# Sums of values in the first attention: rounded operands, values as rounded and remainder columns, two query tiles per matmul

## The reference, cut to what matters

```python
# q, k, v: [1, 512, 16, 64]; for each block of queries, over the keys before its end
log_fail = where(mask, log_sigmoid(-logits), 0.0)
between  = cumsum(log_fail, reverse=True) - log_fail
w        = where(mask, exp(log_sigmoid(logits) + between), 0.0)
out      = einsum('bhqk,bkhd->bqhd', w, v)
...
y_sb = einsum('ble,ed->bld', o * silu(z_sb), w_sb_proj)
```

## Time and profile before

| what | value |
|---|---|
| median of 3 runs | 1355.64 us (1355.26 to 1355.69) |
| profiled execution: its time | 1355.3 us |
| profiled execution: span | 1353.4 us |
| TensorE busy, share of the span | 99% |
| VectorE, ScalarE busy | 60%, 46% |
| attention stage | about 301.6 to 470.8 us |
| granted TensorE clock | 1.00 in all slices |

### The profile page before, as it was taken

One profiled execution on the slowest core, in us unless ns is written; L12 is line 12 of the kernel. 1 busy time (PEld: TensorE's weight loads), 2 busy tenths in 40 slices (PEclk: granted clock), 3 DMA queues, 4 the chain that ended last, 5 costly groups with the idle time before them and its releaser, 6 DMA issues. The chain is left out here.

```text
span 1353.4 us, 17944 instructions
## 1 busy us (share of the span) xinstructions
PE 1338.7 (99%) x6941; PEld 1111.6 (82%) x6941; DVE 818.6 (60%) x1271; ACT 620.9 (46%) x1147; POOL 53.8 (4%) x38
## 2 busy tenths in 40 slices
PE   9999999999999999999999999999999999999998
PEld 7888878888888888888778877888898888888886
DVE  5786654357666544343648876667464565656668
ACT  6554433457767633323526466663443332333333
POOL 0025300000000000000010000000000000000000
PEclk9999999999999999999999999999999999999999
DMA  4222113242111154322261200101425312331321
GB/s 169 85 82 84 63 63 112 90 129 90 32 63 49 56 208 136 106 86 87 73 198 52 84 23 17 32 1 59 151 88 176 135 34 92 134 116 63 104 84 62
DMA packets 33621, 120.67 MB, mean 89 GB/s; under 512 B 3716, under 2 KB 5124, under 8 KB 32258
## 3 DMA queue, kind: packets, MB, share of 16 engines
q1 hardware_dynamic: 32962, 118.48, 26.1%
q10 hardware_dynamic: 576, 1.05, 0.4%
HBM read 112.18 MB, written 4.19 MB: 86 GB/s over the span
## 5 line engine op out<-in xcount | busy, mean ns | idle before, releaser
L1004 PE MATMUL bank<-a_hi,whi 128*128 128x512 f32 (+1 forms) x880 | 346.7, 394 | 0.4 <-DVE a_lo L2402 0.4
L1004 PE MATMUL bank<-a_hi,wlo 128*128 128x512 f32 (+1 forms) x880 | 336.8, 383 | 0.0
L1004 PE MATMUL bank<-a_lo,whi 128*128 128x512 f32 (+1 forms) x880 | 335.9, 382 | 0.0
L1452 ACT ACTIVATE whi<-wraw 128x1024 fp32r<-128x1024 f32 x170 | 175.9, 1055 | 194.2 <-PE bank L1004 125.9
L1835 DVE TENSOR_TENSOR wlo<-wraw,whi 128x1024 fp32r<-128x1024 f32 x170 | 206.9, 1233 | 63.3 <-ACT whi L1452 59.7
L1004 PEld LDWEIGHTS bank<-a_hi,wlo 128*128 128x128 f32 x880 | 165.4, 188 | 33.0
L1004 PEld LDWEIGHTS bank<-a_hi,whi 128*128 128x128 f32 x880 | 165.8, 188 | 31.5 <-issue 2.3
L1004 PEld LDWEIGHTS bank<-a_lo,whi 128*128 128x128 f32 x880 | 165.8, 188 | 31.2 <-issue 1.7
L1004 PE MATMUL bank<-arena 128*128 128x128 f32 (+5 forms) x1332 | 185.9, 285 | 1.9 <-DVE arena L2393 1.1
L1004 PEld LDWEIGHTS bank<-arena 128*128 128x128 f32 (+1 forms) x1332 | 165.0, 191 | 11.8 <-issue 5.3
L1004 PE MATMUL bank<-whi,a_hi 128*128 128x512 f32 x288 | 115.0, 399 | 1.4 <-DVE wlo L1835 0.7
(11 more groups left out here) (269 smaller groups left out, 1838.0 us busy)
## 6 DMA issues: line engine op xcount, KB each, us to landing
wraw<-in_wblk SPq DMA_DIRECT2D x170, 512.0 KB, 3.9
arena<-in_quarters SPq DMA_DIRECT2D x8, 1024.0 KB, 8.4
arena<-in_quarters SPq DMA_DIRECT2D x4, 768.0 KB, 6.3
arena<-in_x SPq DMA_DIRECT2D x4, 512.0 KB, 6.1
arena<-in_x SPq DMA_DIRECT2D x1, 2048.0 KB, 8.2
spill<-arena SPq DMA_DIRECT2D x4, 512.0 KB, 7.5
arena<-spill SPq DMA_DIRECT2D x1, 2048.0 KB, 9.4
out<-arena SPq DMA_DIRECT2D x8, 256.0 KB, 2.0
```

What stands on the lines that cost most here:

```text
L1004: return nc.tensor.matmul(o, lhsT, rhs, start=start, stop=stop, **kw)
L1452: A(whi[n % 2][:, cols], wraw[i][:, 0:cols.stop - cols.start], ACT.Copy).then_inc(s_hi, 1)
```

## The change

The sums of values get rounded operands. For each head the 64 columns of values become 128 columns of weights, 64 rounded and 64 remainder (values_of(h)); the turned weights are split too, into sb_wT_hi, which ScalarE writes with its copy, and sb_wT_lo, which VectorE gets by subtracting it from the same bank. Two query tiles are summed together: in even units of TensorE, function summed does a matmul of 256 columns for every block of keys that both tiles see and one of 128 for the last block, each for hi and lo. The output then has 64 rows from rounded values and 64 from remainders, which ScalarE and VectorE add. TensorE's order in a unit changes: sums, turns, logits. ScalarE copies the turned weights first in a unit, VectorE subtracts first. The turns wait for s_wTlo (VectorE) where they waited for s_wT (ScalarE). The last three units are woven with slices of the first z_sb block. One DMA (the residual) waits for half the count of s_pv, which now counts pairs. Memory places change.

```diff
@@ -227,9 +227,12 @@
     for c in range(NK):
         gs += feature("gate_ssd", [(G0 + P * c, P), (P * c, P)], [("gate", c), ("y_ssd", c)], "AB")
     steps += weave([("sb", u) for u in range(SH * NT)], gs)
-    steps += [("sb", SH * NT + i) for i in range(SB_LAG + 1)]
     for j in range(4):
-        steps += feature("w_in", [(ZS0 + 256 * j, 256)], [("z_sb", 2 * j), ("z_sb", 2 * j + 1)], "AA")
+        zs = feature("w_in", [(ZS0 + 256 * j, 256)], [("z_sb", 2 * j), ("z_sb", 2 * j + 1)], "AA")
+        if j == 0:
+            for i in range(SB_LAG + 1):
+                zs.insert(2 * i + 1, ("sb", SH * NT + i))
+        steps += zs
     for c in range(NK):
         steps += feature("gate_sb", [(G0 + D + P * c, P), (P * c, P)], [("gate2", c), ("y_sb", c)], "AB")
         if 1 <= c <= NK // 2:
@@ -694,8 +697,7 @@
 
         def k_hihi(h):
 
-            i = h // 2
-            kb = (30, 28, 30)[h] if h < 3 else 72 + 2 * (i - 1) if h % 2 else 28 if i == 2 else 72 + 2 * (i - 3)
+            kb = 78 if h >= 13 and h % 2 else 30 - 2 * (h % 2)
             return mem(kb, [T], rounded_arena)
 
         def head_rows(h):
@@ -716,8 +718,18 @@
         ones_r = b_hi[:, 5, 0:P]
         sb_sig = mem(48, [2, T])
         sb_fail = mem(52, [2, T])
-        sb_w = mem(57, [3, T])
-        sb_wT = mem(63, [2, T])
+        sb_w = mem(56, [3, T])
+        sb_wT_hi = mem(64, [NT, 2 * P], rounded_arena)
+        even_values = mem(62, [NT, P], rounded_arena)
+        odd_values = mem(32, [NT, D], rounded_arena)
+
+        def sb_wT_lo(h):
+            return mem(24 if h < SH // 2 else 72, [NT, 2 * P], rounded_arena)
+
+        def values_of(h):
+
+            return odd_values[:, :, P * (h // 2):P * (h // 2) + P] if h % 2 else even_values
+
         v_before = [mem(52, [NT, 512]), mem(16, [NT, 512])]
         small_t = {"dt": mem(12, [T]), "gates": mem(10, [T])}
         tt = mem(48, [2, T])
@@ -829,6 +841,7 @@
         s_dv = sem("s_value_steps")
         s_vs = [sem(f"s_values_shifted{i}") for i in range(2)]
         s_tr, s_wT, s_pv, s_o = sem("s_sb_turned"), sem("s_sb_wT"), sem("s_sb_summed"), sem("s_sb_out")
+        s_orest, s_wTlo, s_vhi, s_vlo = sem("s_sb_out_rest"), sem("s_sb_wT_rest"), sem("s_values_rounded"), sem("s_values_rest")
         s_khi, s_klo, s_kz = sem("s_stacks_rounded"), sem("s_stacks_rest"), sem("s_stacks_zero")
         s_t, s_tround, s_mg = sem("s_product"), sem("s_product_rounded"), sem("s_merged")
         s_res, s_zero = sem("s_residual"), sem("s_zero")
@@ -907,6 +920,19 @@
 
         def norm_no(name, t):
             return APPLIED.index((name, t)) + 1
+
+        def value_head(u):
+
+            if u == 0:
+                return 0
+            return u // NT + 1 if u % NT == NT - 1 and u // NT + 1 < SH else None
+
+        def summed_head(u):
+
+            o = u - SB_LAG - 2
+            if u == SH * NT + SB_LAG:
+                return SH - 1
+            return o // NT if 0 <= o and o % NT == NT - 1 else None
 
         def norm_cols(name, t):
 
@@ -962,7 +988,7 @@
                     sp.wait_ge(s_xd, 2 * NT)
                     sp.dma_start(rows["y"], dram["ssd_norm"]).then_inc(s_row["y"], 16)
                 if n == LATE:
-                    sp.wait_ge(s_pv, SH * NT)
+                    sp.wait_ge(s_pv, SH * NT // 2)
                     sp.dma_start(xres, by_token(dram["x"])).then_inc(s_res, 16)
                     sp.dma_start(npost, dram["norm_post"]).then_inc(s_res, 16)
                 if n == LATE + 2:
@@ -1351,6 +1377,17 @@
                                 .then_inc(s_aux, 1)
 
             def stick(u):
+                v = u - SB_LAG - 1
+                if 0 <= v < SH * NT and v % 2:
+                    summed(*divmod(v, NT))
+                v = u - SB_LAG
+                if 0 <= v < SH * NT:
+                    pe.wait_ge(s_scan, v + 1)
+                    if v >= 1:
+                        pe.wait_ge(s_wTlo, v)
+                    for kb in range(v % NT + 1):
+                        last = nc.tensor.transpose(bank[BANK_WT][:, P * kb:P * kb + P], sb_w[:, v % 3, P * kb:P * kb + P], ident)
+                    last.then_inc(s_tr, 1)
                 if u < SH * NT:
                     h, qt = divmod(u, NT)
                     kend = P * (qt + 1)
@@ -1366,29 +1403,25 @@
                     mm(ps[:, 0:kend], queries, k_hihi(h)[:, 0:kend], True, False)
                     mm(ps[:, 0:kend], queries, k_lo[:, h % 2, 0:kend], False, False)
                     mm(ps[:, kend - P:kend], identb, strict, False, True).then_inc(s_qk, 1)
-                v = u - SB_LAG
-                if 0 <= v < SH * NT:
-                    pe.wait_ge(s_scan, v + 1)
-                    if v >= 1:
-                        pe.wait_ge(s_wT, v)
-                    for kb in range(v % NT + 1):
-                        last = nc.tensor.transpose(bank[BANK_WT][:, P * kb:P * kb + P], sb_w[:, v % 3, P * kb:P * kb + P], ident)
-                    last.then_inc(s_tr, 1)
-                v = u - SB_LAG - 1
-                if 0 <= v < SH * NT:
-                    h, qt = divmod(v, NT)
-                    pair = slice(P * (h // 2), P * (h // 2) + P)
-                    pe.wait_ge(s_wT, v + 1)
-                    if qt == 0:
-                        pe.wait_ge(s_dv, 1 + h // 8)
-                        if h == 1:
-                            pe.wait_ge(*end_sem("v"))
-                        if h >= 2:
-                            pe.wait_ge(s_o, h - 1)
-                    for kb in range(qt + 1):
-                        last = mm(bank[BANKS_STICK[h % 2]][:, P * qt:P * qt + P], vt[:, kb, pair],
-                                  sb_wT[:, v % 2, P * kb:P * kb + P], kb == 0, kb == qt)
-                    last.then_inc(s_pv, 1)
+
+            def summed(h, qt):
+
+                pe.wait_ge(s_wT, NT * h + qt + 1)
+                pe.wait_ge(s_wTlo, NT * h + qt + 1)
+                if qt == 1:
+                    pe.wait_ge(s_vlo, h + 1)
+                    if h == 1:
+                        pe.wait_ge(*end_sem("v"))
+                    if h >= 2:
+                        pe.wait_ge(s_o, h - 1)
+                out_ = bank[BANKS_STICK[h % 2]]
+                passes = [(kb, half) for half in (sb_wT_hi, sb_wT_lo(h)) for kb in range(qt + 1)]
+                passes.append(passes.pop(qt + 1))
+                for n, (kb, half) in enumerate(passes):
+                    first = P if kb == qt else 0
+                    last = mm(out_[:, P * (qt - 1) + first:P * qt + P], values_of(h)[:, kb, :], half[:, kb, first:2 * P],
+                              n == 0, n == len(passes) - 1)
+                last.then_inc(s_pv, 1)
 
             for s in STEPS:
                 if s[0] == "gemm":
@@ -1595,7 +1628,25 @@
                 if i == 2:
                     A(q_hilo[own, h % 2, :], qf[own, h // 2, :], ACT.Copy).then_inc(s_khi, 1)
 
+            def round_values(h):
+
+                if h % 2 == 0:
+                    act.wait_ge(s_dv, 1 + h // NH)
+                    if h >= 2:
+                        act.wait_ge(s_pv, 2 * (h - 1))
+                else:
+                    act.wait_ge(s_vlo, h)
+                A(values_of(h)[:, :, 0:HD], vt[:, :, HD * h:HD * h + HD], ACT.Copy).then_inc(s_vhi, 1)
+
             def stick(u):
+                v = u - SB_LAG
+                if 0 <= v < SH * NT:
+                    kend = P * (v % NT + 1)
+                    act.wait_ge(s_tr, v + 1)
+                    if v >= 2 and v % 2 == 0:
+                        act.wait_ge(s_pv, v // 2)
+                    A(sb_wT_hi[:, 0:v % NT + 1, P * (v % 2):P * (v % 2) + P],
+                      bank[BANK_WT][:, 0:kend].rearrange("p (a b) -> p a b", b=P), ACT.Copy).then_inc(s_wT, 1)
                 if u < SH * NT:
                     kend = P * (u % NT + 1)
                     act.wait_ge(s_qk, u + 1)
@@ -1608,13 +1659,12 @@
                     A(sb_fail[:, u % 2, 0:kend], ps[:, 0:kend], ACT.Sigmoid, scale=-SCALE).then_inc(s_sig, 1)
                     if u % NT < 3 and u // NT + 1 < SH:
                         stack(u // NT + 1, u % NT)
-                v = u - SB_LAG
-                if 0 <= v < SH * NT:
-                    kend = P * (v % NT + 1)
-                    act.wait_ge(s_tr, v + 1)
-                    if v >= 2:
-                        act.wait_ge(s_pv, v - 1)
-                    A(sb_wT[:, v % 2, 0:kend], bank[BANK_WT][:, 0:kend], ACT.Copy).then_inc(s_wT, 1)
+                if value_head(u) is not None:
+                    round_values(value_head(u))
+                h = summed_head(u)
+                if h is not None:
+                    act.wait_ge(s_pv, 2 * h + 2)
+                    A(qf[HD * (h % 2):HD * (h % 2) + HD, h // 2, :], bank[BANKS_STICK[h % 2]][HD:P, :], ACT.Copy).then_inc(s_orest, 1)
 
             def dt_part(i):
 
@@ -1887,6 +1937,10 @@
                     if kind == "y_ssd":
                         if i == 0:
                             dve.wait_ge(s_dv, 2)
```

(26 more changed lines are left out.)

## The result

| | before | after |
|---|---|---|
| median | 1355.36 us | 1362.25 us (1360.98 to 1363.19, 5 runs) |
| ratio | | 1.0049, 95% interval 1.0034 to 1.0064 |
| profiled execution, its span | 1355.3, 1353.4 us | 1363.19, 1361.4 us |
| one round of the attention stage | 21.03 us | 21.51 us |

The account below looks back on a forecast made before the run. TensorE, busy for 99% of the span, was taken as the bound. First round +1.8, six rounds +2.6, last round -0.3, end -1.0, small waits +0.2 gave +3.3 on 1355.3: 1358.6, by the median 1359.0; range 1347 to 1365.

Parts of the forecast that it names:

- that case alone: Attention stage: two waits take back about all of TensorE's gain, round 21.4 against 21.03; 1355 to 1362, chance 0.50.
- TensorE's own work: Attention stage: falls by 0.55 us per head, 1.1 per round; without waits a round would be about 19.7.
- Rival (d): Sums of values: rounded narrow matmuls cost as much as float32 ones, nothing saved; chance 0.20 together with (c).
- VectorE's prices: Subtractions 0.29, 0.42, 0.56, 0.69 for four widths, values' remainder 0.42, addition 0.70; VectorE's sum 18.5 per round.
- The two waits: TensorE's turns wait for VectorE's queued subtraction: 1.05 and 0.63 in units with u % 8 = 5 and 1.
- Early and late starts: VectorE's operations start 0.09 early where operands begin at the same partition as the last ones', 0.03 late elsewhere.
- Rival (c): All VectorE operations held in the attention stage: round 22.0, kernel 1364; chance 0.20 together with (d).
- (a): Attention stage: VectorE keeps up, turns never wait, TensorE stays the bound; round 19.7, kernel 1344; chance 0.10.
- (b): Attention stage: half of the waits gone, a round near 20.6, kernel 1352; chance 0.20.
- First round: Attention stage's start: four more VectorE operations in units 4 to 7; unit 9 starts some 1.8 us later.
- Six rounds: Attention stage's middle: each round 0.4 to 0.45 us longer, +2.6 together.
- End: Units 64 to 66, woven with slices: TensorE needs some 2.4 us in place of 3.4, 1.0 saved.

Follow-up runs that it names:

- experiment 8: The kernel before, with only the remainders of keys and queries moved to GpSimd: 1353.80 us, 0.9989 against before.
- experiment 11: The changed kernel without the sums of the low halves of the turned weights, the low half still made: 1353.27 us, 0.9986 against before.
- Experiments 2: The changed kernel with VectorE subtracting only 8 columns per block and both passes of sums taking the rounded half: 1353.23 us, 0.9985 against before.
- experiments 3: The changed kernel with the values' remainder made by GpSimd in place of VectorE: 1357.16 us, 1.0014 against before.
- experiment 9: The changed kernel, first z_sb tile in bank 0, VectorE's values' and weights' remainders, addition and product queued behind the next unit's subtraction: 1355.25 us.
- experiment 5: The changed kernel with the first z_sb tile summed in bank 0 instead of bank 1: 1358.84 us, 1.0025 against before.
- 12: As experiment 9, with the remainders of keys and queries directly behind the subtraction: 1355.14 us, 0.9997 against before.
- experiment 4: The changed kernel with remainders of values, keys and queries on GpSimd and the last three units before the z_sb slices: 1416.57 us, 1.0449 against before.
- experiment 1: The changed kernel with the last three attention units ahead of the z_sb slices, as before the change: 1363.41 us, 1.0060 against before.
- experiment 6: As experiment 4, but GpSimd asked a unit earlier and the end as in the change: 1365.35 us, 1.0071 against before.

## Why the prediction was right, step by step

**The forecast.** 1359.0 with 1347 to 1365, slower the likeliest: measured 1362.25, slower by 0.5%. The case behind it, TensorE's gain given back in two waits, is the one that came; the time lies just outside the 1355 to 1362 of that case alone, and the end of the stage is the reason.

**TensorE's own work.** Forecast 19.7 per round without waits. The units that don't wait last 2.20, 2.91, 2.20 and 2.46 from bf16 to bf16; twice that is 19.54. A matmul of 128 columns costs 408.55 - 408.29 = 0.26 for two, 0.13: no cheaper than one of 256, as taken. From the bf16 matmul at 408.55 to the slice's second one at 408.90 it is 0.35, 0.12 above the usual 0.23: 0.13 was taken. Rival (d), that the change wouldn't shorten TensorE's work, is out: its work per round fell from 20.81 (the kernel before without its wait, experiment 8) to 19.54, and experiment 11 prices the low half at some 1.5 per round.

**VectorE's prices.** 0.29, 0.42, 0.56 and 0.69 for the subtraction; measured 0.291, 0.424, 0.548 and 0.691. The strided operand cost nothing. Values' remainder 0.40 (0.42), addition 0.68 (0.70). **ScalarE's:** values 0.422 (0.42), the 64 x 512 copy 0.595 (0.59). The sum was too high all the same: VectorE is busy for 17.5 per round (104.84 in the six rounds from slice 9 to 57), not 18.5, since operations that start before the end of the last one count their common time once. The sign "more than 16 in 20" came out at 15.96 to 16.02.

**The two waits.** Forecast 1.05 and 0.63 in units with u % 8 = 5 and 1. From bf16 to bf16 these units last 3.30 and 2.97, against 2.20 for the same unit unhindered: 1.10 and 0.77. Round 21.42 forecast, 21.51 measured. Experiments 2 and 3 show the cause, how soon VectorE's queue comes to the end of the subtraction: taking 0.4 out ahead of it, or making it shorter, takes away the wait by about as much. In experiment 9, where only the order is another, the wait of the turns goes.

**Early and late starts.** The prediction took VectorE's operations to start 0.09 early where operands begin at the same partition as the last ones' and 0.03 late elsewhere. In the second chain above every operation starts early (408.61 against an end at 408.70; 409.53 against 409.61); in the first, whose head has its rows in the other half of the partitions, addition and subtraction start 0.03 late (398.85 against 398.82; 399.56 against 399.53). The prediction counted the operand remainders as late for odd heads only; the queries' remainder, which reads one half of the partitions and writes the other, is late for an even head too (L2413 at 406.68, 0.03 behind the end of the subtraction that starts at 406.23). Rival (c), all operations late, is out.

**Rivals (a) and (b).** (a) asked for turns that never wait; they wait 14 times in 170 us. (b) asked for half the waits; all of 1.7 came, and 1.96 per round counting the 0.09 in units with u % 8 = 4.

**The sum, where two terms were mis-sized.** First round: +1.8 forecast for the start of unit 9. It starts at 324.77 after (its turns) and at 322.63 before (its logits); less the 0.85 that is +1.3. Six rounds: +2.6 forecast, 6 x 0.485 = +2.9 measured, so unit 57 starts 4.2 later. Last round: -0.3 forecast; slice 63 is 3.9 later, so -0.3. End: -1.0 forecast, +3.2 measured. With 0.2 for small waits it is 3.3 forecast, and 7.1 measured.

The step that failed is "with rounded sums and slices between them some 2.4: 1.0 saved". The time of TensorE's own work was right: with the other bank (experiment 5) the end saves 0.8. What I left out is the bank of the first slice. Moving that slice ahead of unit 64 put it right behind the last product of the old block, which shares its bank, and I had not looked for who empties it. Shown by experiment 5: 3.4 us of the medians go with that one bank. Of the 4.0 in the trace 2.26 are the wait itself and about 1.7 the matmuls at 1.2 GHz behind it, and I had forecast no change of the clock at all. The wait comes in every execution, the fall of the clock in three of the five, so that without it the change takes about 1361.2. That the forecast still came within 3.3 us owes something to the first round, taken 0.5 too dear.

**What stays open.** Whether another order of VectorE's queue would give a round near 19.6. Experiment 9 removed the wait of the turns and 12 that of the logits, and neither gave the gain that its expectation promised, because each order of the eight units' work left some operation late. Nor does any run show why the clock falls behind the same idle time in one execution and not in another.

## What to carry to other kernels

A matmul's cheaper form pays only if the engine that prepares its operands hands them over in time, and the busy share doesn't say whether it does: here VectorE was busy for 80% of the time, and an urgent operation of 0.55 us behind 1.1 to 1.75 us of unhurried work cost all that TensorE had gained. Write down each engine's queue around the new wait, unit by unit, before believing a sum. And when a step is moved, look up who empties the bank that it writes: the first matmul after a seam inherits the last reader's place in another engine's queue.

## What the runs showed of the hardware that I had not expected

- TensorE's clock fell to 1.2 GHz behind a single idle time of 2.26 us, in the midst of a stage at the full clock, and 512-column matmuls then started 0.42 to 0.43 apart, from 475.09 to 476.80. Idle times of 2.17 us (experiment 4) and 1.95 us (experiment 1) were followed by the same. But the same 2.26 us left it at 1.00 in the profiles of experiments 3 and 6, and in two of five executions of the change. Idle times of 0.6 to 1.1 us, twice per 21.5 us, left it at 2.4 GHz.
- Work moved from VectorE to GpSimd can cost VectorE more than it saves: 64 x 512 subtractions of 0.69 took GpSimd 1.28 to 1.36 on average (experiment 6) and held a 0.41 scan up to 1.52 and a 1.20 remainder up to 2.32. Where nothing waited for VectorE (experiment 8) the same move gained 1.5 us.
- GpSimd is held in turn: in experiment 8 one of its operations, begun at 395.66 during a weights' remainder that ended at 396.59, took 2.05 in place of 1.29.
